# Early score tiles of a top-16 stage in three fp32r products, and two more of them outside the expert loop

## The reference, cut to what matters

```python
def peer(h, w_q, subkeys, u_tab, v_tab):          # 256 tokens, width 1024
    q = (hf @ w_q).astype(jnp.float32).reshape(t, PEER_HEADS, 2, PEER_QDIM // 2)
    s = jnp.einsum('thsd,hskd->thsk', q, subkeys)
    top_s, top_i = lax.top_k(s, PEER_TOPK)                       # 16 of 128, for 8 heads x 2 sides
    cand_s = top_s[:, :, 0, :, None] + top_s[:, :, 1, None, :]
    ...
    best_s, best_pos = lax.top_k(cand_s.reshape(t, PEER_HEADS, PEER_TOPK * PEER_TOPK), PEER_TOPK)
    gate = jax.nn.softmax(best_s, axis=-1)
    ...
        act = jax.nn.gelu(jnp.einsum('thkd,td->thk', ub, hb).astype(jnp.float32))
        return jnp.einsum('thk,thkd->td', (gb * act).astype(vb.dtype), vb)
```

## Time and profile before

| | |
|---|---|
| median of 3 runs | 2112.27 us (2112.13 to 2113.38) |
| profiled execution | 2111.2 us, span 2109.4 us |
| TensorE busy | 2024.2 us, 96% of the span |
| VectorE busy | 1572.2 us, 75% |
| ScalarE busy | 1081.3 us, 51% |
| GpSimd busy | 258.5 us, 12% |
| mean granted TensorE clock | 0.988 |

### The profile page before, as it was taken

One profiled execution on the slowest core, in us unless ns is written; L12 is line 12 of the kernel. 1 busy time (PEld: TensorE's weight loads), 2 busy tenths in 40 slices (PEclk: granted clock), 3 DMA queues, 4 the chain that ended last, 5 costly groups with the idle time before them and its releaser, 6 DMA issues.

```text
span 2109.4 us, 34074 instructions
## 1 busy us (share of the span) xinstructions
PE 2024.2 (96%) x11188; PEld 1742.2 (83%) x11188; DVE 1572.2 (75%) x3436; ACT 1081.3 (51%) x1703; POOL 258.5 (12%) x309
## 2 busy tenths in 40 slices
PE   4998999999999999999999989999999999999998
PEld 4788989888888888888778989898888888888876
DVE  8883889766788888887656358996676767678854
ACT  3223338654776766666522142585555555554443
POOL 2002439200000000000010043690000000000000
PEclk9999999999999999999999999999999999999998
DMA  9366311355778877555443362114555565555561
GB/s 369 133 261 259 121 54 52 136 180 197 261 290 294 295 280 280 189 180 208 164 168 110 106 244 81 66 64 172 190 188 189 204 214 198 189 188 181 179 233 60
DMA packets 115595, 391.66 MB, mean 186 GB/s; under 512 B 12736, under 2 KB 20800, under 8 KB 115008
## 3 DMA queue, kind: packets, MB, share of 16 engines
q1 hardware_dynamic: 115520, 390.69, 51.9%
HBM read 384.35 MB, written 6.29 MB: 185 GB/s over the span
## 4 chain that ended last, share of the span: by engine, by line
PE 62%; DVE 22%; issue 7%; ACT 3%; DMA 3%; DVEq 1%; SPq 1%; POOL 1%; ACTq 0%
PE ps L868 23%; PE ps L859 12%; PE ps L861 5%; PE ps L613 5%; DVE v_lo L1678 3%; DVE next_w_ada_ring L1723 3%; DVE u_lo L1673 3%; PE ps L626 3%; PE ps L754 2%; DVE onehot_gate L1657 2%; PE ps L830 2%; DMA weight_ring<-in_w_q_dram 2%; DVE gated L1686 2%; ACT gelu L1220 2%; DVE gelu L1682 1%
## 5 line engine op out<-in xcount | busy, mean ns | idle before, releaser
L859 PE MATMUL ps<-h_hi_lo,u_hi 128*128 128x512 f32 x1728 | 629.0, 398 | 8.3 <-DVE u_lo L1673 8.1
L861 PE MATMUL ps<-h_hi_lo,u_lo 128*128 128x256 f32 x1512 | 424.6, 281 | 0.0
L859 PEld LDWEIGHTS ps<-h_hi_lo,u_hi 128*128 128x128 f32 x1728 | 325.2, 188 | 79.0 <-issue 6.5
L861 PEld LDWEIGHTS ps<-h_hi_lo,u_lo 128*128 128x128 f32 x1512 | 286.3, 189 | 8.1
L1673 DVE TENSOR_TENSOR u_lo<-weight_ring,u_hi 128x1024 fp32r<-128x1024 f32 x216 | 263.7, 1222 | 22.0 <-ACT u_hi L1209 18.8
L868 PE MATMUL ps<-v_hi,gated_hi 128*128 128x512 f32 x864 | 272.2, 396 | 5.6 <-DVE gated_lo L1692 4.6
L868 PE MATMUL ps<-v_lo,gated_hi 128*128 128x512 f32 x864 | 268.4, 392 | 0.0
L868 PE MATMUL ps<-v_hi,gated_lo 128*128 128x512 f32 x864 | 266.4, 390 | 0.0
L1678 DVE TENSOR_TENSOR v_lo<-weight_ring,v_hi 128x1024 fp32r<-128x1024 f32 x216 | 263.3, 1219 | 0.5 <-ACT v_hi L1214 0.5
L1214 ACT ACTIVATE v_hi<-weight_ring 128x1024 fp32r<-128x1024 f32 x216 | 227.4, 1053 | 52.8 <-PE ps L868 52.6
L1209 ACT ACTIVATE u_hi<-weight_ring 128x1024 fp32r<-128x1024 f32 x216 | 227.6, 1055 | 4.6 <-DMA weight_ring<-in_u_tab_dram 3.9
(11 more groups left out here) (318 smaller groups left out, 3209.0 us busy)
## 6 DMA issues: line engine op xcount, KB each, us to landing
weight_ring<-in_u_tab_dram SPq DMA_DIRECT2D x224, 512.0 KB, 4.4
weight_ring<-in_v_tab_dram SPq DMA_DIRECT2D x216, 512.0 KB, 3.5
next_w_ada_ring<-in_w_ada_dram SPq DMA_DIRECT2D x56, 512.0 KB, 4.5
weight_ring<-in_w_in_dram SPq DMA_DIRECT2D x46, 512.0 KB, 3.6
w_ada_ring<-in_w_ada_dram SPq DMA_DIRECT2D x40, 512.0 KB, 7.8
v_tail<-in_v_tab_dram SPq DMA_DIRECT2D x40, 512.0 KB, 4.8
weight_ring<-in_w_q_dram SPq DMA_DIRECT2D x32, 512.0 KB, 3.5
u_ahead<-in_u_tab_dram SPq DMA_DIRECT2D x22, 512.0 KB, 8.6
```

Source lines behind the costliest of these rows:

```text
L859: last = mm(both, UH[:, b, k, :], HB[:, :, k, :], start=(k == 0), stop=(k == KT - 1))
L861: mm(PS[:, 4 + b, 0:T], UL[:, b, k, :], HH[:, k, :], start=False, stop=False)
```

## The change

The number of early tiles in the top-16 stage goes from 11 to 13, AHEAD from 20 to 22 and the loop from 108 to 106 experts. The stretch of the loop with `gate_ahead` becomes experts 82 to 103, and the four plain experts behind it fall away.

The early tiles of the top-16 stage are computed as in the loop: ScalarE writes a high part (`ahead_high`, into six places), GpSimd replaces the raw tile by its low part (`ahead_low`), and TensorE does 24 fp32r products with the high and low parts of h. Tiles 11 and 12 are loaded into the places of tiles 0 and 1 once these are used, so two neighbouring places share a semaphore. The kept arrays and some v places get other addresses; two pairs of semaphores of the mixer are merged, without another order.

```diff
-A_TOP = 11
+A_TOP = 13
+A_RING = 11
...
+        HIGH_AT = [0, 1, 0, 1, 0, 1, 2, 3, 4, 5, 0, 1, 2]
+        UAH = [at(f"u_ahead_hi_{i}", o, [P, KT, P], F32R) for i, o in enumerate((0, 1024, 38912, 39936, 40960, 41984))]
...
-        V_AT = (0, 1024, 2048, 3072, 4096, 20480, 21504, 22528, 23552)
+        V_AT = (0, 1024, 2048, 3072, 4096, 22016, 23040, 30720, 31744)
...
+                for a in range(A_RING, A_TOP):
+                    sp.wait_ge(ahead_mm, l * AHEAD + a - A_RING + 1)
+                    early_tile(a)
...
                 def ahead(a):
-                    pe.wait_ge(in_ahead[a], 16 * (l + 1))
-                    if a == 0:
-                        pe.wait_ge(h32_done, l + 1)
+                    pe.wait_ge(ua_split, l * A_TOP + a + 1)
                     if a >= 2:
                         pe.wait_ge(ahead_gelu, l * AHEAD + a - 1)
+                    uh, ul, out = UAH[HIGH_AT[a]], RAWL[a % A_RING], PS[:, 2 + a % 2, 0:T]
                     for k in range(KT):
-                        last = mm(PS[:, 2 + a % 2, 0:T], RAWU[a][:, k, :], H32[:, k, :], start=(k == 0), stop=(k == KT - 1))
+                        mm(out, uh[:, k, :], HH[:, k, :], start=(k == 0), stop=False)
+                        mm(out, uh[:, k, :], HL[:, k, :], start=False, stop=False)
+                        last = mm(out, ul[:, k, :], HH[:, k, :], start=False, stop=(k == KT - 1))
                     last.then_inc(ahead_mm, 1)
...
+                def ahead_low(a):
+
+                    pool.wait_ge(ua_hi, l * A_TOP + a + 1)
+                    gp.tensor_tensor(RAWL[a % A_RING][:, :, :], RAWU[a % A_RING][:, :, :], UAH[HIGH_AT[a]][:, :, :].bitcast(F32),
+                                     ALU.subtract).then_inc(ua_split, 1)
+
                 for n in range(16):
...
+                    if n in (4, 5):
+                        ahead_low(n - 4)
+                    if n - 2 in AHEAD_AT:
+                        ahead_low(AHEAD_AT.index(n - 2) + 2)
+                for a in range(5, A_TOP):
+                    ahead_low(a)
...
+                def ahead_high(a):
+
+                    users = [b for b in range(a) if HIGH_AT[b] == HIGH_AT[a]]
+                    act.wait_ge(*ahead_loaded(l, a))
+                    if users:
+                        act.wait_ge(ahead_mm, l * AHEAD + users[-1] + 1)
+                    elif HIGH_AT[a] >= 2:
+                        act.wait_ge(q_mm, (l + 1) * 16)
+                    else:
+                        act.wait_ge(h_split, (l + 1) * KT)
+                    fn(UAH[HIGH_AT[a]][:, :, :], RAWU[a % A_RING][:, :, :], ACT.Copy).then_inc(ua_hi, 1)
...
+                    if n in (2, 3):
+                        ahead_high(n - 2)
                     if n in AHEAD_AT:
                         gelu_ahead(AHEAD_AT.index(n))
-                gelu_ahead(4)
-                gelu_ahead(5)
+                        ahead_high(AHEAD_AT.index(n) + 2)
+                ahead_high(6)
+                ahead_high(7)
+                for a in range(4, 7):
+                    gelu_ahead(a)
+                    ahead_high(a + 4)
                 act.wait_ge(gate_in, l + 1)
                 fn(GATE[:, :, :], GATE[:, :, :], ACT.Exp).then_inc(gate_exp, 1)
-                for a in range(6, A_TOP):
+                for a in range(7, A_TOP):
                     gelu_ahead(a)
+                    if a + 4 < A_TOP:
+                        ahead_high(a + 4)
...
-                expert_tiles(AHEAD_TILE + AHEAD, NM - 2)
+                assert AHEAD_TILE + AHEAD == NM - 2
```

More of the change, by code:

```diff
@@ L182, in trunk @@
         CBN = at("next_cond", 4096, [P, D])
-        RAWU = [at(f"u_ahead_{a}", 2560 if a == 10 else 19200 + 1024 * a, [P, KT, P]) for a in range(A_TOP)]
+        AHEAD_FROM = [19200 + 1024 * a for a in range(A_RING - 1)] + [2560]
+        RAWU = [at(f"u_ahead_{a}", o, [P, KT, P]) for a, o in enumerate(AHEAD_FROM)]
+        RAWL = [at(f"u_ahead_lo_{a}", o, [P, KT, P], F32R) for a, o in enumerate(AHEAD_FROM)]
+        HIGH_AT = [0, 1, 0, 1, 0, 1, 2, 3, 4, 5, 0, 1, 2]
+        UAH = [at(f"u_ahead_hi_{i}", o, [P, KT, P], F32R) for i, o in enumerate((0, 1024, 38912, 39936, 40960, 41984))]
         GEA = at("gelu_ahead", 29440, [P, A_TOP, T])
@@ L190, in trunk @@
         GER = at("gelu_back", 5120, [P, AHEAD, T])
[L191 to L193 removed]
+        GHA = at("gated_ahead_hi", 10752, [P, AHEAD, T], F32R)
+        GLA = at("gated_ahead_lo", 16384, [P, AHEAD, T], F32R)
+        V_AT = (0, 1024, 2048, 3072, 4096, 22016, 23040, 30720, 31744)
         RAWV = [at(f"v_tail_{a}", o, [P, D]) for a, o in enumerate(V_AT)]
@@ L262, in trunk @@
         h_hi = sem("h_hi_done")
-        rvar = sem("ret_var_done")
-        rstd_done = sem("ret_std_done")
-        mvar = sem("merge_var_done")
-        mstd = sem("merge_std_done")
+        mvar = sem("head_and_merge_var_done")
+        mstd = sem("head_and_merge_std_done")
         h_split = sem("h_split_done")
@@ L338, in trunk @@
         s_sum = sem("expert_scores_summed")
-        in_ahead = [sem(f"u_ahead_loaded_{a}") for a in range(A_TOP)]
+        in_ahead = [sem(f"u_ahead_pair_loaded_{a}") for a in range((A_RING + 1) // 2)]
         in_late = [sem(f"u_ahead_late_loaded_{i}") for i in range(2)]
@@ L346, in trunk @@
         h32_done = sem("h_fp32_done")
+        ua_hi = sem("u_ahead_hi_done")
+        ua_split = sem("u_ahead_split")
         ahead_mm = sem("ahead_scores")
@@ L374, in trunk, with ahead_loaded @@
         LATE_STORES = [len(range(i, A_GATE, 4)) for i in range(4)]
+        def ahead_loaded(l, a):
+            pair = a % A_RING // 2
+            tiles = [b // A_RING for b in range(A_TOP) if b % A_RING // 2 == pair]
+            return in_ahead[pair], 16 * (l * len(tiles) + sum(b <= a // A_RING for b in tiles))
         TILE_IN, TILE_OUT, TILE_Q = 0, IN_TILES, IN_TILES + KT
@@ L436, in _, with early_tile @@
                         ada(m)
+                def early_tile(a):
+                    sp.dma_start(RAWU[a % A_RING][:, :, :], u_tab[l, NM + a].rearrange("p (k n) -> p k n", n=P)).then_inc(
+                        in_ahead[a % A_RING // 2], 16)
                 def ahead_late(i):
@@ L470, in _ @@
                         sp.wait_ge(ada_used, N_ADA)
-                        for a in range(A_TOP):
-                            sp.dma_start(RAWU[a][:, :, :], u_tab[l, NM + a].rearrange("p (k n) -> p k n", n=P)).then_inc(in_ahead[a], 16)
+                        for a in range(A_RING):
+                            early_tile(a)
                         ahead_late(0)
@@ L835, in ahead_step @@
                     if k == 0:
+                        if i == 0:
+                            pe.wait_ge(h32_done, l + 1)
                         pe.wait_ge(in_late[i % 2], 16 * (len(range(i % 2, A_GATE, 2)) * l + i // 2 + 1))
@@ L1120, in _ @@
                 fn(PT[:, :, :], ps[:, 0:18 * P].rearrange("p (n k) -> p n k", k=P), ACT.Copy).then_inc(pt_ev, 1)
-                act.wait_ge(rvar, l + 1)
-                fn(SM[:, 3, :], SM[:, 3, :], ACT.Sqrt).then_inc(rstd_done, 1)
-                act.wait_ge(mvar, l + 1)
+                act.wait_ge(mvar, 2 * l + 1)
+                fn(SM[:, 3, :], SM[:, 3, :], ACT.Sqrt).then_inc(mstd, 1)
+                act.wait_ge(mvar, 2 * l + 2)
                 fn(RMS[:, :], RMS[:, :], ACT.Sqrt).then_inc(mstd, 1)
@@ L1546, in _ @@
                 v.tensor_scalar(RMS[:, 0:2], RMS[:, 0:2], 1.0 / AW, EPS, ALU.mult, ALU.add).then_inc(mvar, 1)
-                dve.wait_ge(rstd_done, l + 1)
+                dve.wait_ge(mstd, 2 * l + 1)
                 link(v.reciprocal(SM[:, 3, :], SM[:, 3, :]))
-                dve.wait_ge(mstd, l + 1)
+                dve.wait_ge(mstd, 2 * l + 2)
                 link(v.reciprocal(RMS[:, :], RMS[:, :]))
```

5 lines of the change are left out of this document (2 added, 3 removed).

## The result

The changed kernel takes 2141.55 us (median of 4 runs, 2137.26 to 2146.81) against 2112.82 us (4 runs, 2112.13 to 2117.26) of the kernel before in the same job: ratio 1.0133, 95% interval 1.0105 to 1.016. Its profiled execution took 2140.02 us; its span is 2138.2 us, 28.8 us longer than that of the kernel before.

What follows compares the result with a forecast made beforehand. TensorE was taken to bound the kernel, except VectorE late in the top-16 stage (after 265 us in layer 0). -10.0 + 2 x 7.8 = +5.6 us on 2111.2 gave 2116.8; runs' median 1.1 higher: 2117.9 us, range 2102 to 2136.

Steps and rivals of the forecast that it cites:

- (1): Expert loop and tail: 106 experts for 108, 22 tail tiles for 20; -5.1 and -5.0 us per layer, -10.0 in all.
- (2): Top-16 stage, TensorE: an early tile takes 2.88 us for 3.46; four where TensorE sets the time give -2.3 us per layer.
- (3): Top-16 stage: high parts 1.05 us on ScalarE, low parts 2.4 on GpSimd; product 5 +1.5 us, later low parts in gaps.
- the ring: Top-16 stage, first to sixteenth query copy: turns of 13.81 us set by TensorE, VectorE idle 2.28 each; blocking costed at nothing.
- (4): Top-16 stage: VectorE waits for GpSimd's low parts at shared ports; 6.9 + 1.7 - 0.8 = +7.8 us per layer.
- the ranking: Top-16 stage, sixteenth query copy to ScalarE's read of the picks (30.9 us): VectorE sets the time, ending 7 to 9 us later.
- Rival B: Top-16 stage: GpSimd gets in between every two VectorE operations; +20 us per layer, 2142; sign: turns of 15 us or more; chance 0.18.

Runs made afterwards that it cites:

- experiment four: Changed kernel with the odd query tiles' top scores copied to PSUM, where VectorE's candidate additions read their second operand; 2124.96 us, ratio 1.0045.

## Why the prediction was wrong

- (1) Right in kind, 1.4 and 0.7 us short: -5.1 and -5.0 us per layer expected, -3.7 and -4.3 measured. The tail is 5.5 us longer as worked out (2 x 2.786); the 1.4 us missing in layer 0 lie in the loop ahead of the kept gelus (expert 81's low part of V comes 1.5 us later after the loop's first than before), and why is open.
- (2) and (3) Right where nothing blocks: the ring's last two turns in layer 0 of the changed kernel, up to the thirteenth and the sixteenth query copy, take 13.2 and 13.3 us for 13.8. With GpSimd's work whole and the additions unblocked (experiment four) the ring takes 65.2 us, 1.0 less than before the change; 0.8 was expected (2.3 less 1.5). High part 1.05 and low part 2.4 us were right too. "Later low parts stand in gaps of GpSimd" was not, at the start: six stand in a row there.
- (4) The mechanism was right, its size was not: +7.8 us per layer expected, +19.8 and +19.2 measured. This is the step that failed, in two of its sentences. "The low parts inside the ring I cost at nothing: the additions of candidates come there before VectorE's idle 2.28 us, which hides one block" failed on the first turn, where GpSimd has six low parts in a row and one burst met four of them, 7.4 us more than alone. Five of the eleven later bursts cost 1.1 to 2.2 us each, 8.9 in all, and the idle time of 8.7 us could not pay for both. The ring lost 5.8 and 5.0 us, and VectorE came out of it 1.9 us in arrears in layer 0. In the ranking "one blocks for 1.0 us and the other between 0 and 2.3", 1.7 us for the additions, was too little: two bursts there lost 6.3 and 1.7 us, 8.0 in all. The rank operations lost 4.2 where I had 6.9, two blocks for three. "The only blocks in the trace last just as long as the rest of one low part" was true of a trace in which GpSimd never had a second low part ready when a burst came: it priced one operation's wait, not a burst's.
- Rival B had the mechanism, with a chance of 0.18: "GpSimd gets in between every two operations of VectorE", +20 us per layer, 2142. The turns of layer 0's ring up to the seventh and the tenth query copy took 16.3 and 17.5 us (14.5 and 13.8 before), which was its sign. I held the ring's idle time against it, which in truth only took 8.7 us off 27.2. That its figure meets the measured one to a microsecond is luck in part: it counted thirteen blocks, one for each new low part, and 30.6 - 8.4 - 0.8 is 21.4, not 20; the trace has fifteen, nine on new low parts and six on those of the query weights, 28.5 us in all.

The Trainium skill's rule (page "SBUF — State Buffer", section "Who interferes with whom") says that an operation with two SBUF inputs contends with a GpSimd instruction that reads and not with one that only writes, and that one with a single SBUF input contends only in a two-port mode, which copies, casts and scalar operations can enter. The runs agree: rank operations of 0.42 us took 2.5 beside subtractions and 1.14 beside copies, 32-wide additions 232 ns beside fills and 188 with an operand in PSUM, and a cast, a scalar operation and a copy of one operand 2.35 to 2.5 us.

## What to carry to other kernels

Before work is moved to GpSimd, count the operations on VectorE with two SBUF operands, and the casts, copies and scalar operations, that are due while GpSimd has a queue: beside back-to-back GpSimd instructions each of them costs up to a whole GpSimd instruction, however small it is, and only VectorE's own idle time pays any of it back. Count GpSimd's old instructions too: a VectorE that is late meets those that it used to miss. Moving the GpSimd work in time does not help if another burst stands there; putting one small operand into PSUM, or sparing GpSimd the tiles that fall into the dense stretch, does. Look also at what is held up behind VectorE: here TensorE's clock fell after it had had little to do, and products behind that ran 0.21 us apart for 0.12. And when a trace shows one instance of contention, ask whether the aggressor had a second instruction ready in it.
